# The order of transposes, activations and product down in the experts' loop of a streaming encoder step

## The reference, cut to what matters

```python
h2 = rms_norm(x) * (1.0 + sc2) + sh2
# hier_moe: the best group, then the best two of its four experts, with weights `combine`
hid = jax.nn.silu(jnp.einsum('nd,edf->nef', t, w_gate)) * jnp.einsum('nd,edf->nef', t, w_up)
out = jnp.einsum('nef,efd->nd', hid * combine[..., None].astype(hid.dtype), w_down)
x = x + g2 * out
```

## Time and profile before

| what | value |
|---|---|
| median of three runs | 1587.72 us (1584.13 to 1591.67) |
| the profiled execution | 1587.63 us |
| its span | 1585.9 us |
| mean granted clock of TensorE, whole span | 0.938 |
| TensorE busy | 1376.0 us (87%) |
| VectorE, ScalarE, GpSimd busy | 770.6, 458.6, 178.2 us |
| `gate_up` matmuls, 416 | 185.1 us busy |
| `down` matmuls, 208 | 93.6 us busy |

### The profile page before, as it was taken

One profiled execution on the slowest core, in us unless ns is written; L12 is line 12 of the kernel. 1 busy time (PEld: TensorE's weight loads), 2 busy tenths in 40 slices (PEclk: granted clock), 3 DMA queues, 4 the chain that ended last, 5 costly groups with the idle time before them and its releaser, 6 DMA issues. The chain is left out here.

```text
span 1585.9 us, 20591 instructions
## 1 busy us (share of the span) xinstructions
PE 1376.0 (87%) x7461; PEld 798.6 (50%) x7462; DVE 770.6 (49%) x1683; ACT 458.6 (29%) x989; POOL 178.2 (11%) x366
## 2 busy tenths in 40 slices
PE   3899997979999899999689998899943999999960
PEld 2555553656644566666456665544423454444430
DVE  0421224868496798889755563423344111111118
ACT  3321112232455466663235551011110111111110
POOL 0000002022010111112100000000001223222220
PEclk9999997989989999999899999999975999999985
DMA  8400016752131442230130003522348468775728
GB/s 323 170 3 4 31 51 156 220 174 31 26 86 38 143 133 74 69 124 29 64 131 1 1 1 142 169 97 86 113 143 298 156 219 276 262 272 196 264 95 321
DMA packets 138826, 205.85 MB, mean 130 GB/s; under 512 B 27205, under 2 KB 102917, under 8 KB 138533
## 3 DMA queue, kind: packets, MB, share of 16 engines
q1 hardware_dynamic: 122524, 160.08, 30.9%
q0 software_dynamic: 10272, 32.49, 5.7%
q10 hardware_dynamic: 5946, 12.15, 2.3%
HBM read 158.71 MB, written 43.98 MB: 128 GB/s over the span
## 5 line engine op out<-in xcount | busy, mean ns | idle before, releaser
L2233 PE MATMUL ps<-ex_wgu,ex_xT 128*128 x416 | 185.1, 598 | 4.0 <-ACT ex_xT L2272 2.5
L1390 DVE TENSOR_SCALAR_CACHE_REDUCE tk_eq<-sc,tk_cand 128x512 bf16<-128x512 f32 (+4 forms) x155 | 146.8, 1007 | 0.0
L2233 PEld LDWEIGHTS ps<-ex_wgu,ex_xT 128*128 128x128 f32 x416 | 77.8, 192 | 93.1 <-issue 93.1
L1788 PE MATMUL ps<-hT,mergedT 128*128 128x512 f32 (+1 forms) x288 | 120.1, 600 | 4.9 <-DMA op_wr<-in_w_route_expert 4.9
L1324 PE MATMUL ps<-zT,gt_w 128*128 128x352 f32 (+1 forms) x384 | 120.9, 468 | 0.0
L1324 PE MATMUL ps<-hT,gt_w 128*128 128x352 f32 (+1 forms) x336 | 105.8, 468 | 0.0
L2306 DVE SCALAR_TENSOR_TENSOR ex_hid<-ex_silu,ex_weight,ps 128x256 f32<-128x256 f32 x26 | 12.5, 480 | 185.0 <-ACT ex_silu L2278 185.0
L1324 PEld LDWEIGHTS ps<-zT,gt_w 128*128 128x128 f32 x384 | 73.0, 190 | 44.1
L2254 PE MATMUL ps<-ex_wd,ex_hidT 128*128 x208 | 93.6, 593 | 0.2 <-DVE ex_hidT L2313 0.2
L1353 ACT ACTIVATE mask<-sc,tk_cand 128x384 bf16<-128x384 f32 (+1 forms) x62 | 82.3, 1329 | 15.0 <-DVE tk_cand L1406 15.0
L1788 PEld LDWEIGHTS ps<-hT,mergedT 128*128 128x128 f32 (+1 forms) x288 | 50.9, 186 | 68.4 <-issue 62.7
(11 more groups left out here) (468 smaller groups left out, 2134.1 us busy)
## 6 DMA issues: line engine op xcount, KB each, us to landing
ex_wgu<-in_w_gate SPq DMA_DIRECT2D x16, 1024.0 KB
ex_wgu<-in_w_up SPq DMA_DIRECT2D x16, 1024.0 KB
ex_wd<-in_w_down SPq DMA_DIRECT2D x16, 1024.0 KB
sp_ada_w<-in_w_ada SPq DMA_DIRECT2D x9, 1024.0 KB
cb_y<-y_dram ACTq DMA_DIRECT2D x16, 512.0 KB, 7.6
merge_left_dram<-qiT SPq DMA_DIRECT2D x8, 544.0 KB, 6.1
mg_gb<-gate_b_dram SPq DMA_DIRECT2D x8, 544.0 KB, 3.8
mergedT<-merge_left_dram SPq DMA_DIRECT2D x8, 544.0 KB, 4.7
```

Source lines behind the costliest of these rows:

```text
L1390: return v.tensor_scalar(junk[j], m.sc[0:r, c:c + w], scalar, 0.0, op, ALU.add, accum_out=cnt[0:r, j:j + 1])
L1788: i = nc.tensor.matmul(m.ps[rows, 2 * (t % 2) + n, :], m.mergedT[:, k, t * P:t * P + r], m.wout[:, k, n * 512:(n + 1) * 512], start=k == 0 ...
L2233: j = nc.tensor.matmul(m.ps[:, 2 + b, :], xT[:, b, k, :], wgu[:, bass.ds(at, 1), k, :].rearrange("p o n -> p (o n)"), start=k == 0, stop=k ...
```

## The change

On TensorE, `transposes(i + 1, b)` moves from the end of a tile's turn to directly behind `gate_up(i, b)`, ahead of the `down` of the tile before. On ScalarE and VectorE the copies of those transposes, `xts(i + 1, b)`, move ahead of `rows` of the tile before to match. `hidden_transposes(i, b)` comes last. GpSimd's and SP's streams are not touched, nor is any instruction's shape.

```diff
@@ TensorE @@
                 def body(i):
                     for b in range(2):
                         gate_up(i, b)
+                        transposes(i + 1, b)
                         previous(down, i, b)
                         hidden_transposes(i, b)
-                        transposes(i + 1, b)
@@ ScalarE @@
                 def body(i):
                     for b in range(2):
                         silu(i, b)
+                        xts(i + 1, b)
                         previous(rows, i, b)
-                        xts(i + 1, b)
```

## The result

The changed kernel takes 1646.08 us (median of 4 runs, 1642.15 to 1654.75) against 1589.27 for the kernel before (median of 4, 1584.13 to 1591.67). The profiled execution has a span of 1646.7 us.

What follows compares the result with a forecast made beforehand. The prediction took TensorE to bound the experts' stretch, busy 300.42 of 306 us. Its terms, 49 + 7 + 12 - 3.6 - 0.5 + 0.9 = 64.8 us on 1587.63, gave 1652 us, range 1627 to 1677.

Steps and rivals of the forecast that it cites:

- The mechanism: Experts' tile loop: the gather is still issued after the preceding down, so transposes wait; a tile takes landing time plus 7.56 us.
- Stalls: TensorE's row transposes wait for the gather, landing time minus 3.83 us in each of 24 tiles: +49 us (+33 to +52).
- the eight gathers: About eight gathers behind a gate and up load may land in near 4.3 to 4.5 us; 3 us off in all.
- The sequencer: TensorE's queue, blocked at a wait, cannot run ahead to register loads: 0.3 us behind each of 24 waits, +7 us.
- The gaps that vanish: Three TensorE gaps of 1.2 us, behind gathers of over 8 us, absorbed by the new waits: -3.6 us.
- The clock: TensorE's clock drops after some waits in the experts' stretch: eight times 1.5 us, +12 us (0 to +36).
- The five pay surely: The five transposes waits over 4 us, over 5 us without a product, each lose clock, 1.5 us apiece.
- Head and tail: Head: transposes cover part of tile 0's wait for activations, -0.5 us; tail: last down loses the transposes in between, +0.9 us.
- The signs that were named: Expected in the new trace: 45 to 52 us of transposes waits, gate_up period about 13.6 us, clock 0.93 to 0.97.
- C: Rival: every tile's wait costs TensorE's clock, +36 us in place of 12, 1675 us (1665 to 1690); chance 0.13.
- D: Rival: gathers land within 3.83 us of issue, only the gaps vanish, 1584.4 us, not slower; chance 0.03.
- B: Rival: landings shorten, restart bubble hides, only the five long waits lose clock, 1632 us (1620 to 1641); chance 0.22.

Runs made afterwards that it cites:

- e1: The changed kernel, but GpSimd issues the gather of tile n+3 ahead of the scatter of tile n-1: 1589.85 us, ratio 1.0016.
- e11: The kernel before, with only TensorE's row transposes moved ahead of the hidden transposes, still behind down: 1588.97 us, ratio 1.0014.
- e8: e1 plus SP signalling an expert's weights behind the next expert's gate and up loads, not behind its down load: 1583.39 us, ratio 0.9972.
- e2: The kernel before, with GpSimd issuing the gather of tile n+3 ahead of the scatter of tile n-1: 1583.49 us, ratio 0.9972.
- e7: The kernel before, without the weight loads of experts 3 to 15 and SP's waits for them: 1583.86 us, ratio 0.9974.
- e6: The changed kernel, without the weight loads of experts 3 to 15 and SP's waits for them: 1601.05 us, ratio 1.0081.
- e9: The changed kernel with 12 empty GpSimd additions ahead of each gather: 1668.35 us, ratio 1.0495.

## Why the prediction was right, point by point

- **The mechanism held**: the gather's issue did not move, its customer did, and the transposes wait in 24 tiles. e1 settles the cause: with the gather released earlier the same order costs 0.16%. e11 shows the other half: without passing down the move costs nothing.
- **Stalls**, forecast +49. By start times the transposes wait 40.7 us, and 4.6 us of lateness went in ahead of them as SP waits, which the gather's wait would otherwise have held: 45.3. The term was 4 us too big, since the 24 landings shortened from 144.0 to 137.8 us, by 6.2 and not the 3 allowed. The place was foreseen: the eight gathers named as following a load of gate and up account for 5.3 of the 6.2 us (41.5 to 36.2).
- **SP's signal** was not foreseen: down's end, SP's down load and then the signal follow one another, and at six tiles gate_up starts 0.75 to 0.85 us late. In the changed kernel this adds nothing, since the gather is landing meanwhile and the transposes wait for it all the same; e1 shows it, 4.6 us by start times, and e8 removes it.
- **The sequencer**, forecast +7. Down starts 0.92 or 1.12 us behind the transposes where the work is 0.87, 3.1 us in all, and its first matmuls run 0.05 to 0.1 us late, 1.7 us: 4.8. The reading of the three gaps as the blocked queue, not as the loop's head alone, is borne out: e2 and e7, with the old order and no late gather, have none. What in the sequencer takes the 1.2 us is not shown.
- **The gaps that vanish**, forecast -3.6: by start times they were 1.36, 1.70 and 1.48 us, so -4.5.
- **The clock**, forecast +12 for eight tiles at 1.5 us. Four tiles lost it, at 2.0 us each: +8.1. These are four of the five waits over 3 us. "The five pay surely" held for four, and none of the shorter ones paid, where three were taken. So a wait in every tile was not enough: 20 of the 24 kept the full clock. The windows of one that lost it:

```profile
1357.50:1359.40 1.90, 1.80 (x9) 1.81 (x10) 0.65 (x1) 0.00 (x0) 0.00 (x0) 0.50 1.09 357
1359.40:1361.50 2.10, 2.10 (x4) 0.97 (x4) 0.04 (x1) 0.59 (x1) 0.00 (x0) 0.50 0.24 74
1361.50:1365.00 3.50, 3.50 (x7) 1.29 (x6) 0.00 (x0) 0.00 (x0) 0.00 (x0) 0.70 0.00 0
```

- **Head and tail**, forecast -0.5 and +0.9: measured -0.3 and +0.9, and 0.2 us more between the first transposes and the first gate_up.
- **The signs that were named**: the gather's issue at 3.1 us, no landing under 3.9 us and the stretch's clock (0.97) came as written, the mean period was 13.9 us for "about 13.6". The sum of the waits did not: 40.7 us by start times (36.2 by the profile's brackets) where 45 to 52 were named.

The sum is 45.3 + 4.8 + 8.1 - 4.5 - 0.3 + 0.9 + 0.2 = 54.5 against 54.1 measured in the stage and 64.8 forecast. The 10 us are three terms that were each sized somewhat high: stalls by 4, sequencer by 2, clock by 4. That the profiled run came within 4 us of the forecast is in part luck: 5.4 us from stages that the change does not touch made up for half of what the sum had too much. Of the rivals, C (clock at every wait) and D (punctual gathers) are excluded by the trace; B was nearer on the clock (four tiles, where it had five), but the five slow gathers did not shorten (8.0 to 9.0 us, before 7.9 to 8.6), and the restarts behind the waits did show.

## What to carry to other kernels

Before moving a consumer forward, find what releases its transfer: if that is the step it is moved past, the time to land shrinks by that step in each turn (here from 8.45 to 3.93 us), and no later turn gives it back. Ask on which side of the releasing step the wait will lie. Behind it, what a late tile waits is time that the next transfer gains; ahead of it, every tile pays. The cheap repair is in the issuing queue, where a gather should not stand behind a scatter that waits for the same step.

## What the runs showed of the hardware that was not expected

- A gather of 512 KB behind a scatter of 512 KB landed in 4.2 to 4.6 us without other traffic (e6), in the changed kernel in 5.4 to 6.3 with a 1 MB load issued 2.9 us ahead and in 8.0 to 9.0 with 3 MB issued within 3 us ahead. Additions of 1.8 us ahead of it (e9) brought the median from 5.5 to 4.4: part of a delay was made up by a shorter landing.
- TensorE kept full clock behind a wait of 3.14 us (1447.14) and lost it behind 3.42 (1357.60). Another tile waited 3.19 us (1526.40) and its down took 5.38 us instead of 3.65. The length of the wait alone does not decide it in this range.
